# Unused TensorE products in the waits of a two-block transformer kernel, and its first mixer's chunk sums reordered

## The reference

```python
for layer in range(2):                       # first block
    mod = silu(c) @ ada_w[layer] + ada_b[layer]          # 6 x 1024: shifts, scales, gates
    h = rms_norm(x, norm1_g[layer]) * (1 + sc1) + sh1
    mix = even_mixer(h, ...) if layer == 0 else odd_mixer(h, ...)
    x = x + g1 * mix
    h = rms_norm(x, norm2_g[layer]) * (1 + sc2) + sh2
    x = x + g2 * grouped_moe(h, router_w, router_b, w_gate, w_up, w_down)   # 16 experts, 4 groups
for layer in range(2):                       # second block
    y = even_mixer_2(...) if layer == 0 else diff_mixer(...)
    x = x + rms_norm(y, g[1])
    x = x + rms_norm(memory_cross_attention(rms_norm(x, g[2]), mem_n, ...), g[3])
    x = x + rms_norm(swiglu(rms_norm(x, g[4]), wg, wu, wd), g[5])
```

## Time and profile before

| what | value |
|---|---|
| runs | 1957.28, 1953.47, 1947.68 us (median 1953.47) |
| profiled execution | 1948.25 us, its span 1946.5 us |
| TensorE busy | 1739.3 us, 89% of the span, 9198 products |
| weight loads of TensorE busy | 1446.0 us, 74% |
| VectorE, ScalarE busy | 1264.2 us, 1073.7 us |
| mean granted TensorE clock | 0.93 of full speed |
| read from HBM | 410.87 MB, mean 212 GB/s |

### The profile page before, as it was taken

How to read it: one execution, slowest core, us unless ns; L and a number is a source line. 1 busy time by engine, 2 the same in 40 slices (tenths; PEclk the granted TensorE clock), 3 DMA queues, 4 the chain that set the end, 5 groups by cost and what they waited for, 6 DMA issues and landing times.

```text
span 1946.5 us, 26378 instructions
## 1 busy us (share of the span) xinstructions
PE 1739.3 (89%) x9198; PEld 1446.0 (74%) x9198; DVE 1264.2 (65%) x1999; ACT 1073.7 (55%) x1649; POOL 13.8 (1%) x29
## 2 busy tenths in 40 slices
PE   5989669999997997799999999877999897679998
PEld 4766468888885865688888678566999775569997
DVE  5686658889885765589889653755544555555454
ACT  2443237878873354578878553555444454554443
POOL 1000000000000000000000000000000000000000
PEclk9899779999998998799999998787999998879999
DMA  9876728999993845399999644122556561215652
GB/s 351 311 242 212 232 87 305 332 351 361 318 352 126 314 131 173 105 354 349 329 355 353 229 146 130 44 87 65 183 185 194 165 202 58 87 44 174 188 179 86
DMA packets 217282, 413.04 MB, mean 212 GB/s; under 512 B 13120, under 2 KB 69488, under 8 KB 216800
## 3 DMA queue, kind: packets, MB, share of 16 engines
q1 hardware_dynamic: 214176, 400.74, 59.9%
q0 software_dynamic: 1904, 8.26, 1.3%
q10 hardware_dynamic: 1120, 2.97, 0.4%
HBM read 410.87 MB, written 1.05 MB: 212 GB/s over the span
## 4 chain that ended last, share of the span: by engine, by line
PE 81%; DVE 10%; ACT 5%; issue 2%; DMA 1%; DVEq 0%; ACTq 0%; SPq 0%
PE banks L721 21%; PE banks L723 21%; PE banks L722 21%; PE banks L967 2%; DVE weights_low L2036 2%; PE banks L770 2%; PE banks L1052 2%; PE banks L1103 1%; PE banks L743 1%; DVE row_gains L2307 1%; PE banks L865 1%; DMA weight_ring<-in_ada_w 1%; ACT scratch L1636 1%; DVE x_state L2162 1%; ACT weights_high L1485 1%
## 5 line engine op out<-in xcount | busy, mean ns | idle before, releaser
L2036 DVE TENSOR_TENSOR weights_low<-weight_ring,weights_high 128x1024 fp32r<-128x1024 f32 (+1 forms) x656 | 771.1, 1217 | 193.9 <-ACT weights_high L1485 108.4
L721 PE MATMUL banks<-weights_high,features_parts 128*128 128x512 f32 (+1 forms) x1488 | 599.0, 403 | 29.7 <-DVE features_parts L2469 8.2
L722 PE MATMUL banks<-weights_low,features_parts 128*128 128x512 f32 (+1 forms) x1488 | 587.1, 395 | 0.0
L723 PE MATMUL banks<-weights_high,features_parts 128*128 128x512 f32 (+1 forms) x1488 | 586.9, 394 | 0.0
L1765 ACT ACTIVATE weights_high<-weight_ring 128x1024 fp32r<-128x1024 f32 x384 | 391.0, 1055 | 106.2 <-PE banks L723 82.5
L721 PEld LDWEIGHTS banks<-weights_high,features_parts 128*128 128x128 f32 x1488 | 286.0, 192 | 96.3 <-issue 20.0
L723 PEld LDWEIGHTS banks<-weights_high,features_parts 128*128 128x128 f32 x1488 | 284.6, 191 | 61.2
L722 PEld LDWEIGHTS banks<-weights_low,features_parts 128*128 128x128 f32 x1488 | 285.6, 192 | 56.6 <-issue 1.0
L1485 ACT ACTIVATE weights_high<-weight_ring 128x1024 fp32r<-128x1024 f32 (+1 forms) x176 | 176.8, 1044 | 154.3 <-PE banks L723 88.5
L721 PE MATMUL banks<-features_parts,weights_high 128*128 128x256 f32 x736 | 210.6, 286 | 0.2
L722 PE MATMUL banks<-features_parts,weights_high 128*128 128x256 f32 x736 | 208.5, 283 | 0.0
(11 more groups left out here) (368 smaller groups left out, 1588.1 us busy)
## 6 DMA issues: line engine op xcount, KB each, us to landing
weight_ring<-in_exp_w_gate SPq DMA_DIRECT2D x128, 512.0 KB, 4.9
weight_ring<-in_exp_w_up SPq DMA_DIRECT2D x128, 512.0 KB, 4.9
weight_ring<-in_exp_w_down SPq DMA_DIRECT2D x128, 512.0 KB, 5.0
weight_ring<-in_ada_w SPq DMA_DIRECT2D x96, 512.0 KB, 5.5
weight_ring<-in_ffn_wg SPq DMA_DIRECT2D x44, 512.0 KB, 4.1
weight_ring<-in_ffn_wu SPq DMA_DIRECT2D x44, 512.0 KB, 4.6
weight_ring<-in_ffn_wd SPq DMA_DIRECT2D x44, 512.0 KB, 4.2
weight_ring<-in_even_w_in SPq DMA_DIRECT2D x28, 512.0 KB, 5.6
```

The costliest lines, as they stand in the source:

```text
L721: eng.matmul(dst, lh, rh, start=first, stop=False, **kw)
L722: eng.matmul(dst, lh, rl, start=False, stop=False, **kw)
L723: mm = eng.matmul(dst, ll, rh, start=False, stop=last, **kw)
L2036: V(half_of(low(s), i, size), half_of(slot(n), i, size), half_of(high(s), i, size).bitcast(F32), ALU.subtract)\
```

## The change

A tile `FILL` of 128 x 128 ones is copied once by VectorE. `stay_busy(bank, count)` issues `count` products of it with itself, 512 columns wide, into a PSUM bank that holds nothing at the time; nobody reads them. It is called ahead of waits of TensorE: with 13, 21 or 13 before normalised states, 12 in `features_of_x`, 4, 13, 8, 11 and 8 in the expert stage, by the table `idle` in the attentions (at its end, at step 1, at steps 2 to 5, and at the last step), 15 and seven times 3 in `differences` and 22 behind it, and at some smaller places. In `differences` the wait for the copied transposes now stands ahead of the wait for the joined probabilities. Before the first transposes there are two new waits, for ScalarE's copy of a chunk and for `FILL`.

In the first mixer chunk 6 moves from behind group 3 to behind group 4, chunks 7 and 8 to behind 5 and 6, and 9 also behind 6. VectorE sums 9 ahead of the attention, 11, 13 and 15 in its steps 0, 1 and 2 rather than 0, 2 and 4; TensorE does the modulations 7 to 15 rather than 8 to 15 in and before the attention, two of them in steps 0 and 2, and the last in step 3 rather than after it.

```diff
@@ -33,7 +33,7 @@
-ADA_EVEN, ADA_A0, ADA_ODD, ADA_A1 = (0, 1, 3, 4, 5, 6), 6, 4, 4
+ADA_EVEN, ADA_A0, ADA_ODD, ADA_A1 = (0, 1, 4, 5, 6, 6), 6, 4, 4
 ADA_ON_PE = (10, 12, 14)
@@ -144,8 +144,7 @@
         group("even_in", "act")
-        if j in ADA_EVEN:
-            ada(1)
+        ada(ADA_EVEN.count(j))
     ada(ADA_A0)
@@ -236,6 +235,7 @@
         FLAG = sb("overflow_flag", [128, 2], I32)
+        FILL = sb("fill", [128, 128], F32R)
         ident, ones = CS[:, 0:128], CS[:, 256:384]
@@ -322,6 +322,7 @@
         ret_values, ret_squared = sem("retention_values"), sem("retention_squared")
+        fill_ready = sem("fill_ready")
         stick_consts, stick_scored, stick_log = sem("stick_consts"), sem("stick_scored"), sem("stick_log1p")
@@ -442,6 +443,7 @@
                 self.scale = 1.0 if name == "a0" else HD ** -0.5
+                self.idle = {"a0": (8, 0, 3, 0), "b0": (5, 4, 4, 0)}.get(name, (4, 11, 3, 0))
                 self.items = [self.item(i, P) for i in range(count)]
@@ -652,8 +654,7 @@
                 group(st["even_in"][j][0], a["even_w_in"][0], 512 * EVEN_ORDER[j])
-                if j in ADA_EVEN:
-                    ada()
+                ada(ADA_EVEN.count(j))
             ada(ADA_A0)
@@ -732,11 +733,19 @@
-            def turn(name, source, parts=128):
+            def stay_busy(bank, count):
+
+                for _ in range(count):
+                    eng.matmul(B[bank][:, :], FILL[:, :], FILL[:, :].unsqueeze(1).to_broadcast([128, 4, 128]),
+                               start=True, stop=True, skip_group_check=True)
+
+            def turn(name, source, busy=()):
...
                     x = first + i
+                    if i >= 4 and busy:
+                        stay_busy(4, busy[i - 4])
                     if x >= 4:
@@ -793,6 +802,7 @@
                 for tb in range(TB):
+                    stay_busy(0, 0 if tb else 12)
                     normed_n[0] += 1
@@ -851,9 +861,9 @@
-                j, bank = 8 + x, 6 + x % 2
+                j, bank = 7 + x, 6 + x % 2
                 if x >= 2:
-                    eng.wait_ge(mod_taken, 8 + x - 1)
+                    eng.wait_ge(mod_taken, 7 + x - 1)
                 if j not in ADA_ON_PE:
@@ -868,11 +878,12 @@
-            def turn_normed(name):
-
+            def turn_normed(name, before=0, busy=()):
+
+                stay_busy(0, before)
                 normed_n[0] += 1
                 eng.wait_ge(normed, normed_n[0])
-                turn(name, lambda i, tb: NB[:, tb, i * 128:(i + 1) * 128])
+                turn(name, lambda i, tb: NB[:, tb, i * 128:(i + 1) * 128], busy)
@@ -894,6 +905,8 @@
                         d, u = pairs.items[t - 2], u0 + t - 2
+                        if t == n + 1:
+                            stay_busy(0, pairs.idle[3])
                         for e in range(2):
@@ -913,6 +926,8 @@
                         u = u0 + t - 1
+                        if t <= 5:
+                            stay_busy(4, pairs.idle[min(t, 2)])
                         for e in range(2):
@@ -922,6 +937,7 @@
                     between(t)
+                stay_busy(4, pairs.idle[0])
@@ -950,9 +966,10 @@
                         h = t - 1
-                        eng.wait_ge(diff_joined, 2 * (h + 1))
                         if h >= 2:
                             eng.wait_ge(diff_copied, h - 1)
+                        stay_busy(4 + h % 2, 3 if h else 15)
+                        eng.wait_ge(diff_joined, 2 * (h + 1))
                         for i in range(3):
@@ -1060,7 +1077,10 @@
                                         start=(k == 0), stop=(k == KD - 1))
+                    if tb == 0:
+                        stay_busy(0, 4)
                 mm.then_inc(router_ready, 1)
+                stay_busy(0, 13)
                 hot = ST[:, 256:264].rearrange("p (t g) -> p t g", t=TB)
@@ -1072,7 +1092,9 @@
                 base = st[f"moe{l}"]
+                stay_busy(0, 8)
                 gather(5 * l)
+                stay_busy(0, 11)
                 eng.wait_ge(backs_copied, 5 * l + 1)
@@ -1081,6 +1103,7 @@
                 used.n += PASSES * PASS_TILES
+                stay_busy(2, 8)
                 eng.wait_ge(moe["y_taken"], PASSES * (l + 1) + 1)
@@ -1131,7 +1154,9 @@
             eng.wait_ge(mod_taken, 4)
-            turn_normed("a0h1")
+            eng.wait_ge(copied["act"], chunks[4]["done"])
+            eng.wait_ge(fill_ready, 1)
+            turn_normed("a0h1", busy=(9, 3, 3, 3))
             P0 = pview(EVEN_IN)
@@ -1164,9 +1189,11 @@
-                if j in (1, 2, 4, 5):
+                if j in (1, 2, 5):
                     modulation((2, 3))
                 if j == 3:
+                    eng.wait_ge(mod_taken, 6)
+                    stay_busy(2, 4)
                     eng.wait_ge(a0_rotated, 1)
@@ -1174,7 +1201,7 @@
                         turn_a0(4 + x, 2048 + 256 * x)
-                    eng.wait_ge(mod_taken, 8)
+                    eng.wait_ge(mod_taken, 7)
                     eng.wait_ge(a0_taken, 4)
@@ -1197,8 +1224,9 @@
                     modulate_a0(2)
+                    modulate_a0(3)
                 if t == 1:
-                    modulate_a0(3)
+                    modulate_a0(4)
                     eng.wait_ge(a0_mixed, 1)
@@ -1207,27 +1235,29 @@
                             mm.then_inc(feature_turned, 2)
-                    modulate_a0(4)
+                    modulate_a0(5)
                     features_wait(RET_HEADS)
+                if t == 2:
+                    modulate_a0(6)
+                    modulate_a0(7)
                 if t == 3:
-                    modulate_a0(5)
-                    modulate_a0(6)
+                    modulate_a0(8)
             attention(Pairs("a0", P0), in_a0)
-            modulate_a0(7)
-            ada[0] += 2 + ADA_A0
+            ada[0] += 3 + ADA_A0
             eng.wait_ge(mod_taken, 16)
...
             project("even_out")
-            turn_normed("a0h2")
+            turn_normed("a0h2", 13)
             turns_taken("a0h2")
...
-            turn_normed("a1h1")
+            turn_normed("a1h1", 21, (2, 2, 2, 2))
             project("odd_in", fresh=by_pair, between=lambda j: modulation((2, 3)) if 2 <= j else None)
...
             eng.wait_ge(copied["act"], chunks[st["odd_in"][-1][1][-1]]["done"])
+            stay_busy(0, 4)
             turn("a1qk", lambda i, tb: P1[:, tb, i * 128:(i + 1) * 128])
@@ -1259,6 +1289,8 @@
                 if t >= 2:
+                    if t == STICKS + 1:
+                        stay_busy(0, 10)
                     eng.wait_ge(stick_probs, t - 1)
@@ -1271,10 +1303,11 @@
                     modulation((7,))
+            stay_busy(0, 11)
             eng.wait_ge(mod_taken, 24)
...
             project("odd_out")
-            turn_normed("a1h2")
+            turn_normed("a1h2", 13)
             turns_taken("a1h2")
@@ -1450,6 +1484,7 @@
             differences(P3)
+            stay_busy(4, 22)
             eng.wait_ge(b1_mixed, 1)
@@ -2548,6 +2583,7 @@
             eng.wait_ge(consts_loaded, CONSTS)
+            eng.tensor_copy(FILL[:, :], ones).then_inc(fill_ready, 1)
             take_turned("mem0", feature, lambda i: (GM[:, 10, i:i + 1], None))
@@ -2567,8 +2603,8 @@
             def in_even(j):
-                if j in (1, 2, 4, 5):
-                    ada_take((0, 4, 5, 0, 6, 7)[j], (2, 3))
+                if j in (1, 2, 5):
+                    ada_take((0, 4, 5, 0, 0, 6)[j], (2, 3))
                 if j == 2:
@@ -2601,13 +2637,15 @@
             def take_a0(x):
-                ada_take(8 + x, (6 + x % 2,), room)
+                ada_take(7 + x, (6 + x % 2,), room)
+            ada_steps(KD)
             take_a0(0)
...
                 if t == 0:
+                    take_a0(2)
                     root(8)
@@ -2619,23 +2657,22 @@
                 if t == 1:
-                    take_a0(2)
+                    take_a0(3)
                     for i in range(2):
...
                         V(hl, B[2 + i][:, :], hh.bitcast(F32), ALU.subtract).then_inc(features_split, 2)
-                    take_a0(3)
-                if t == 2:
                     take_a0(4)
                     ada_steps(KD)
+                if t == 2:
+                    take_a0(5)
+                    take_a0(6)
+                    ada_steps(KD)
+                if t == 3:
+                    take_a0(7)
                 if t == 4:
-                    take_a0(5)
-                    ada_steps(KD)
-                if t == 5:
-                    take_a0(6)
-                if t == 6:
-                    take_a0(7)
+                    take_a0(8)
             attention(Pairs("a0", P0), (), in_a0)
...
             add_projected("even_out", 0)

```

## The result

The median of the changed kernel is 1932.78 us (1928.21 to 1938.03, 4 runs) against 1953.55 us (1947.68 to 1957.28, 4 runs) for the kernel before. The ratio is 0.9908, 95% interval 0.9884 to 0.9931: faster, by 18 us in the middle of the interval, and under 2%; the time lies outside the forecast's range of 1862 to 1925.

The account below looks back on a forecast made before the run. TensorE was taken to bound the kernel, slowed by its clock falling to 1.2 GHz after waits. Terms summed to 76 us, less 14 for waits left open: 62 off 1948.25 gives 1886, plus 2, 1888 us; range 1862 to 1925.

Parts of the forecast that it names:

- Part (a) of the first mixer: Moved chunk sum removes most of TensorE's 7.72 us wait behind group 3: gain 6, and 1 for the low clock.
- 131 ns per product: Skill's rate for sustained 512-column products, an estimated 53 us for the 406; the forecast used the trace's 0.23 us instead.
- part (b) of the first mixer: In the first mixer's attention, each VectorE sum starts one step earlier: gain 6.5 us, bounds 0 and 12.
- rival (4): Waits fed by loads or VectorE take up TensorE's gain, uncovered fills eat the rest: near 1945 us; chance 7%.
- about 32 of them: Unused products counted as uncovered by any wait, out of 406, priced at 0.23 us each.
- Rival (3): Slower: fills do not lift the clock and each lasts 0.43 us: 1982 us; chance 3%.
- The 14 us that I took off: Deducted from the 76 us sum: seven clock falls in waits left partly idle cost 12, fills ending late 2.
- the cross attentions: Two cross attentions: first two waits, on other engines' softmax, stay; TensorE's steps between them gain 6 us each, 12.
- x transposed six times: Fills before L770 lift the clock for 16 transposes and the products behind: about 2 us each, 12 in all.
- The 3 us forecast at the start of the first mixer: Fills of 9, 3, 3, 3 at the start gain 3 us in the products after them.
- the end of the differences: Heads paced by ScalarE, so gain only at the stage's two ends: 4 us together, lower bound minus 4.
- Rival (1): Clock falls between the fills, so terms of transposes and small products halve, about 27 us lost: 1915 us; chance 27%.

Follow-up runs that it names:

- e1: The changed kernel with `stay_busy` issuing nothing, the new order of modulation steps and the extra waits kept: 1947.03 us, ratio 0.9975.
- e9: The changed kernel itself, profiled once more with nothing altered: 1930.90 us, against 1938.03 in its first profile.
- e3: The changed kernel with TensorE's modulation chunk 7 issued between the halves of projection group 6, ahead of the retention values: 1919.99 us, ratio 0.9851.
- e4: The changed kernel without 48 unused products that have little or no wait to lie in: 1922.28 us, ratio 0.9856.
- e8: The changed kernel with e3's edit and e4's (but 12-item attention's 20 fills kept), plus longer fills and some new ones: 1904.09 us, ratio 0.9766.
- e12: e8 plus one unused product behind every second router product, 7 between each router's products: 1908.12 us, ratio 0.9786.
- e6: The changed kernel with e3's and e4's edits (12-item attention's 20 fills kept), without the 13 fills behind the router, twice: 1923.41 us, ratio 0.9866.

## Why the prediction was wrong

**Right.** The direction, and what bounds the kernel. The fills slow nobody on other engines (VectorE is busy for 1264.0 us, 1264.2 before; ScalarE for 1072.8, 1073.7 before). The product behind a closed wait runs at the forecast's speed: gathering 3.84 us, the scatterings -1.7 each, the first expert products -2.7 and -1.6, the second mixer's output -1.6 (forecast with its wait: -2.5). Part (a) of the first mixer, the wait behind group 3, was worth 9.0 us (8.3 in e1) for 7 forecast. The 131 ns per product of the Trainium skill ("TensorE: Matmul & The Clock Gate", section Back-to-back issue gap) play no part in any of it: 12 fills at the high level take 2.88 us (shown below), 0.24 each.

**The step that failed first: part (b) of the first mixer.** I wrote that "VectorE does the moved sum while TensorE finishes", and followed the loads and the banks step by step, but not the accumulator that the sum writes. The sum waited for TensorE's own later step, and the attention took 9 us more (6 in e9's profile) rather than 6.5 less: 13 to 16 us of the miss. e3, which moves nothing but that one step, shows how much of it is the dependence: 9.5 us (6.6 against e9). The other 6.0 were a gain that was not there. In e3 the waits of 7.04 and 5.3 us are gone and TensorE's waits in the stage come to 10.9 us for 19.9, but it is busy for 48.6 us instead of 41.2, and the stage is only 0.5 us shorter. What the 7.4 us of busy time are, fills beside the moved work or a slower pace, was not separated. The lower bound of 0 that I set for (b), "the sums only change places in VectorE's line", was no bound, since a sum brought forward on VectorE had become dependent on one that TensorE does later. No sign that I had named stood for it: for rival (4) I looked for a new wait on VectorE at the first expert products only, and this one, 4.73 us, stands ahead of the first mixer's attention.

**The price of the uncovered fills.** The forecast counted about 32 of them at 0.23 us; e4 takes out 48. Many stand in stretches of small work where the clock is low, cost 0.43 to 0.45 each there, and drag with them the covered fills behind, as the 13 at the router show. The stages of routing, the second mixer and the compression are 15 us shorter in e4's profile than in the changed kernel's (the medians are 10.5 us apart). Rival (3) had the price right, but as a failure everywhere; it is one of certain places.

**The waits left half open.** The 14 us that I took off for this were the right thought and too small in one place, the cross attentions: 12 forecast, 2.4 found, 8.6 with the waits closed. I had written that the first two waits "stay"; they do, but the one of 2.27 us got no fill and lets the clock fall. Behind rests of 1.89 and 2.27 us the clock fell; with 1.02 and 0.43 us, in e8, it did not. The length of the rest doesn't settle it alone. Ahead of the x transposes of the changed kernel a rest of 2.19 us was followed by no fall and rests of 1.92 and 1.91 us by one within 2 us; a rest of 1.27 us, ahead of a feed-forward, was followed by a fall in e9's profile and by none in the first. In e8's profile, where the rests at these places are 1.06 us at most, there is none.

**Clock-bound that was not.** For x transposed six times I took 2 us each. TensorE ahead of a feed-forward, before:

```profile
1346.39 3.64 PE L770 MATMUL banks<-projected,x_state 128*128 128x128 f32 x16 [3.96 <-DVE projected L2169]
```

and in the changed kernel:

```profile
1334.86 2.88 PE L739 MATMUL banks<-fill 128*128 128x512 f32 x12
1339.02 1.16 PE L779 MATMUL banks<-projected,x_state 128*128 128x128 f32 x8 [1.28 <-DVE projected L2204]
1340.63 1.16 PE L779 MATMUL banks<-projected,x_state 128*128 128x128 f32 x8 [0.45 <-DVE projected L2204]
```

The 16 transposes come down from 3.64 to 2.32 us of work, but between the halves TensorE now waits 0.45 us for VectorE, and 0.5 us more at the end for the first split: 0.4 us are won. The slow transposes had hidden VectorE's second half. And the products behind them had been at the high clock already in the kernel before: 0.12 us apart at 1350.38. That holds ahead of the two feed-forwards behind the cross attentions; at the other four places the low clock had reached into them, by 0.5 to 2.5 us. The term was mis-sized by 9.3 us. With the waits closed (e8) it comes to 5.0, so 2.3 us of the miss are waits left open and 7.0 are this. The 3 us forecast at the start of the first mixer went the same way: in e8 the first transposes and the first projection run at 1.00 throughout and take 56.7 us, 0.9 of them fills, for 55.7 before, where 10.2 us of them were low; TensorE now waits 2.2 us for VectorE's low parts. At the end of the differences (4 forecast for both ends, 0.1 found) it is different: there the clock fell behind the fills all the same (a rest of 3.34 us is left), and the first products start 0.43 us apart, as before.

**The rivals.** Rival (4), 1945 us, was nearest in number, 12 us off, and had 7%. It said that waits fed by VectorE take up the gain and uncovered fills eat the rest, and both are shown, though not at the first expert products, where I looked for them. Rival (1), "the clock falls between the fills", 1915 us, was 18 us off. Its mechanism is shown in part (the cross attentions; the routers). The rule that I cited beside it, that transposes do not count as work for the clock (the Trainium skill, "TensorE: Matmul & The Clock Gate", Part 4: PE-mode transpose), would fit e12's second router, which came right behind transposes and fell 2.0 us after its start; it doesn't explain e12's first, behind the same transposes, which stayed at 1.00.

## What to carry to other kernels

Before a step is moved to an engine's idle time, list everything that it waits for, the buffer that it writes included: the one dependence overlooked here turned a gain of 12 us into none. Fill a wait with unused work only where it is a wait, nearly to its end, and where what follows is bound by the clock: here rests of 1.1 us at most held the clock in the cross attentions and ahead of the x transposes, and rests of 1.3 to 2.3 us held it in some executions and places and not in others. A fill without a wait costs its length, 0.23 us here, at the lower clock about twice that. Price each such term by asking what would pace the work if it ran at the high clock, and look whether it didn't already.

## What was not expected of the hardware

The place where the clock falls, and above all the one where it comes back, differs in small work from one execution of the same program to the next (e9). Over several kernels the 12-item attention with the same instructions took 63.8 to 70.3 us.

A second scatter lies ahead of any fill, in the first 32 products of the memory projections. They took 7.14 us in e6 and in the kernel before, 8.98 in the changed kernel and 9.54 in e1, which has no fill at all. That stage and the first transposes behind it take 42.1 to 42.2 us in the kernel before and in e6 to e9, and 44.0 to 44.6 in the others. Two rows, the kernel before and the changed one, the columns as in the earlier trace rows:

```profile
25.90:30.00 4.10, 4.08 (x19) 3.63 (x20) 3.79 (x6) 0.35 (x1) 0.00 (x0) 1.00 1.07 371
```

```profile
25.90:30.00 4.10, 4.10 (x11) 3.30 (x12) 3.79 (x6) 0.00 (x0) 0.00 (x0) 1.00 1.06 370
```

Both say 1.00, but one has 19 products in the 4.10 us and the other 11. The 1.00 is not a reading: the trace's record of the clock starts only at 25.4 us in the kernel before and at 29.6 in the changed one, and ahead of it the profile prints 1.00 even while TensorE has not begun. The first 16 transposes, at 21.6 us, take 3.65 us in both, the time of the low level and not of the high one. So TensorE starts at 1.2 GHz and comes up at one time or another. In all fourteen profiles the short stage goes with a first record at 25.1 to 26.3 us and the long one with a first record at 29.6 to 32.0. It is worth up to 2.4 us, and the comparison of the first profiles, before and changed, holds 1.8 us of it.

And in e8 a TensorE that was busy for 10.50 of 10.50 us, with the router's 16-column products and fills behind them, was granted 0.67.
